# Sliding-window attention in a two-layer hybrid decoder step: TensorE's order of scores and probability transposes within a round

## Chip, cores, metric

One core of one Trainium2 chip. The metric is device microseconds of one launch of the whole kernel, median of the runs.

## What is computed

One inference step of a trunk of two layers (DEPTH = 2, D_MODEL = 1024). Layer 0 is grouped-query attention over a window of 128 keys, 16 query heads on 4 key heads of 64, with a learned sink per head, RMS-normed queries and keys and a relative-position bias. Layer 1 is an mLSTM. Each is followed by a squared-ReLU MLP of width 4096. The prompt has 16 meta tokens and 1024 tokens; a sample group has 8 sequences of 4 tokens with 128 cached keys and values each. The part that matters here:

```
s = einsum('...qkgd,...skd->...kgqs', qg, k) * hd**-0.5 + rel_bias(dist)
m = maximum(max(s), sink);  p = exp(s - m)
den = sum(p) + exp(sink - m)
o = einsum('...kgqs,...skd->...qkgd', (p / den), v)
```

Everything is float32; the large projections split each operand into a high and a low part (three matmuls in the place of one).

## The kernel before

All of it is one program on one core, with a hand-written instruction list for each engine and semaphores between them. The stages follow one another: load and norm, q/k/v projection, attention, output projection (`wo_pe`), MLP, mLSTM, MLP, store.

**The rounds.** Prompt attention has NG = 36 pieces, numbered n = 0 to 35: four steps of four heads each, and in each step nine query blocks (`block_of`, L732). Block 0 of a step is the 16 meta tokens (16 x 16 scores a head), block 1 sees 16 + 128 keys, the seven others are full: 128 queries by 256 keys a head. Below, S(n), T(n) and V(n) are TensorE's three kinds of work on piece n:

- S(n), `att_scores_pe` (L742): scores of four heads into PSUM banks 0/1 for even n, 2/3 for odd n. It first waits for `s_taken`: the softmax of piece n-2 has read these banks.
- T(n), `att_transpose_pe` (L763): eight transposes of the scaled probabilities into banks 4 and 5, which exist once. It waits for `prob_ready` of n and for `pT_ready` of n-1.
- V(n), `att_values_pe` (L777): sixteen matmuls probabilities times values into bank 6 or 7. It waits for `o_taken` of n-2 and for `pT_ready` of n. In rounds up to n = 8 it also carries two other transposes (`turns_pe`).

LAG = 4: in round n TensorE (`att_pe`, L814) issues T(n-4), S(n), V(n-5), in this order. The rounds run from 2 to 40; S(0) and S(1) come earlier, from `att_first_pe`. The two kinds of exception: T(0) stands behind S(4); and the sample group's cached keys are transposed in rounds 36 and 37 (`turn_k_pe` 0 and 1, then 2 and 3, L1005, four transposes each into banks 0 and 1), there behind T. Turns 2 and 3 wait until turns 0 and 1 have been copied out (`k_copied`), because they use the same banks. In round 38 `sample_scores_pe` (L1042) follows, behind T(34).

**The other engines, in order in round n.** VectorE (`att_dve`, L939): o(n-6), the two operations that take V(n-6)'s result (L907, L910, which signals `o_taken`); softmax(n), four score reads (L846, the last signals `s_taken`) and a sum (L852); den(n-1), sum and reciprocal (L871, L873). Softmax(n) waits for S(n) and, because the four probability buffers go round, for T(n-4). In round 18 `spread_dve` (L990) stands first. ScalarE (`att_act`, L919): pT(n-4), the copy of T(n-4) to SBUF (L890; L893 and L894 for small blocks), which signals `pT_ready`; exp(n-1), four exponentials and one for the sinks (L862, L864). In round 36 turn 1's copy follows exp(35) (L1025), and turn 0's copy follows den(35) on VectorE (L1020). GpSimd: the scaling by 1/den (L880), which signals `prob_ready`.

Behind attention `wo_pe` (L1169) waits for the last `o_taken`, does two groups of the projection, the transposes of the sample probabilities, another group, and then `sample_values_pe` (L1107): matmuls with 32 columns each (L1117), and the rest of the projection.

Of the kernel before, what the change touches and what calls it, by code (L numbers as in the profile page):

```python
# [137 lines left out]
def build(nc, a, out, scratch):  # L138

    with ExitStack() as ctx:  # L140
# [562 lines left out]
        NG = 4 * TILES  # L703
        P_BUFS = 4
        LAG, READY = 4, 2
# [20 lines left out]
        def prob_of(n, rows, k, cols):  # L726

            if n == 0:
                return prob_m[rows, k, cols.start - BLK:cols.stop - BLK]
            return (prob_1 if n == 1 else prob[p_buf(n)])[rows, k, cols]  # L730

        def block_of(n):  # L732

            step, b = divmod(n, TILES)
            if b == 0:
                return (COL_M, META), (0, None, 0), BLK, BLK + META, step
            col = BLK * (b - 1)
            if b == 1:
                return (col, BLK), (COL_M, None, META), BLK - META, 2 * BLK, step
            return (col, BLK), (col - BLK, b - 2, BLK), 0, 2 * BLK, step  # L740

        def att_scores_pe(pe, n):  # L742
            (qc, nq), (pc, _, npk), k0, k1, step = block_of(n)
            gp, ip = divmod(step, 2)
            if n >= 2:
                pe.wait_ge(s_taken, n - 1)
            for i in range(2):
                for par in range(2):
                    rows = slice(HD * par, HD * par + HD)
                    bank = 2 * (n % 2) + par  # L750
                    lhsT = q[rows, 4 * gp + 2 * ip + i, qc:qc + nq]
                    o = ps[0:nq, bank, 2 * BLK * i:2 * BLK * i + 2 * BLK]
                    if npk == BLK:
                        last = nc.tensor.matmul(o, lhsT, kn[rows, gp, pc:pc + 2 * BLK], start=True, stop=True)  # L754
                    else:
                        if npk:
                            nc.tensor.matmul(o[:, k0:BLK], lhsT, kn[rows, gp, pc:pc + npk],
                                             start=True, stop=True)
                        last = nc.tensor.matmul(o[:, BLK:k1], lhsT, kn[rows, gp, qc:qc + nq],
                                                start=True, stop=True)  # L760
            last.then_inc(s_done, 1)

        def att_transpose_pe(pe, n):  # L763
            (qc, nq), (pc, _, npk), k0, k1, step = block_of(n)
            pe.wait_ge(prob_ready, n + 1)
            if n >= 1:
                pe.wait_ge(pT_ready, n)
            for k in range(4):
                bank = 4 + k // 2
                for part, (c0, nk) in enumerate(((k0, npk), (BLK, nq))):  # L770
                    if nk:
                        o = ps[0:nk, bank, (k % 2) * 2 * BLK + part * BLK:][:, 0:nq]
                        last = nc.tensor.transpose(o, prob_of(n, slice(0, nq), k, slice(c0, c0 + nk)),  # L773
                                                   ident[0:nq, 0:nq])
            last.then_inc(t_done, 1)

        def att_values_pe(pe, n):  # L777
            (qc, nq), (pc, pt, npk), k0, k1, step = block_of(n)
            b = n % TILES
            gp, ip = divmod(step, 2)  # L780
            if n >= 2:
                pe.wait_ge(o_taken, n - 1)
            turns_pe(pe, n)
            if n == 0:
                pe.wait_ge(vmeta_done, 1)
            if n == 2 * TILES:
                pe.wait_ge(v_taken, V_TAKEN)
                pe.wait_ge(vmeta_done, 2)
            pe.wait_ge(pT_ready, n + 1)
            for i in range(2):  # L790
                for part, (t, nk) in enumerate(((pt, npk), (b - 1 if b else None, nq))):
                    for par in range(2):
                        cols = slice((2 * gp + par) * HD, (2 * gp + par) * HD + HD)
                        o = ps[HD * par:HD * par + HD, 6 + n % 2, BLK * i:BLK * i + nq]
                        v = v_tok[:, t, cols] if t is not None else v_meta[:, cols]
                        if nk:
                            last = nc.tensor.matmul(o, v, probT[0:nk, n % 2, 2 * par + i, part, 0:nq],  # L797
                                                    start=part == 0 or npk == 0, stop=part == 1)
            last.then_inc(pv_done, 1)
# [13 lines left out]

        def att_pe(pe):  # L814
            for n in range(2, NG + LAG + 1):
                if LAG < n < NG + LAG:
                    att_transpose_pe(pe, n - LAG)
                if NG <= n < NG + 2:
                    turn_k_pe(pe, 2 * (n - NG))
                    turn_k_pe(pe, 2 * (n - NG) + 1)  # L820
                if n == NG + 2:
                    sample_scores_pe(pe)
                if n == 3 * TILES:
                    pe.wait_ge(qk_normed, 30)
                if n < NG:
                    att_scores_pe(pe, n)
                if n == LAG:
                    pe.wait_ge(qk_ln, 30)
                    pe.wait_ge(out_free, V_LAST + 1)
                    att_transpose_pe(pe, 0)  # L830
                if n > LAG:
                    att_values_pe(pe, n - LAG - 1)

# [171 lines left out]
        def turn_k_pe(pe, j):  # L1005

            if j == 0:
                pe.wait_ge(kc_in, 64)
                pe.wait_ge(s_taken, NG - 1)
            elif j == 2:  # L1010
                pe.wait_ge(k_copied, 2)
            for i in range(4):
                b = 4 * (j % 2) + i
                last = nc.tensor.transpose(ps[:, j % 2, P * i:P * i + P],
                                           k_raw[:, b, P * (j // 2):P * (j // 2) + P], ident)
            last.then_inc(s_turns, 1)
# [25 lines left out]
        def sample_scores_pe(pe):  # L1042

            pe.wait_ge(s_taken, NG)
            pe.wait_ge(k_copied, 4)
            pe.wait_ge(q_spread, 5)
            for t in range(4):
                for c, ncol, keys in ((0, WIN, lambda gp, b: kcT[:, gp, b, :]),
                                      (WIN, SAMPLE, lambda gp, b: kn[:, gp, COL_S:COL_M])):
                    for gp in range(2):  # L1050
                        for half in range(2):
                            b = 2 * t + half
                            c0 = 256 * (t % 2) + c
                            o = ps[64 * half:64 * half + 64, 2 + t // 2, c0:c0 + ncol]
                            last = nc.tensor.matmul(o, q_big[:, gp, b, :], keys(gp, b), start=gp == 0, stop=gp == 1)
            last.then_inc(s_turns, 1)
# [1395 lines left out]
        @block.tensor  # L2452
        def _(pe):
            load_pe(pe)
            pe.wait_ge(gains_in, 48)
            pe.wait_ge(x_by_dve, 8)
            nc.tensor.transpose(ps[:, 7, 0:5 * KC], gain_rows[:, :], ident[0:5 * KC, 0:5 * KC]
                                ).then_inc(gains_t, 1)
            pe.wait_ge(line_in, 64)
            pe.wait_ge(rel_one, 1)  # L2460
            pe.wait_ge(x_by_act, 8)
            nc.tensor.matmul(ps[0:QH, 6, 0:LINE], rel_ext[:, :], bucket[:, :], start=True, stop=True
                             ).then_inc(line_mm, 1)
            qkv_pe(pe)
            att_pe(pe)
            wo_pe(pe)
            first_up_pe(pe, 0, U_MLP0, N_MLP0, h_hi, h_lo)
            mlp_slice_pe(pe, 0, U_MLP0, N_MLP0, 0, h_hi, h_lo, 1)
            with pe.Fori(1, SLICES) as i:
                mlp_slice_pe(pe, 0, U_MLP0, N_MLP0, i, h_hi, h_lo)  # L2470
            gates_pe(pe)
            in_pe(pe)
            chunks_pe(pe)
            out_pe(pe)
            first_up_pe(pe, 1, U_MLP1, N_MLP1, h_hi2, h_lo2)
            mlp_slice_pe(pe, 1, U_MLP1, N_MLP1, 0, h_hi2, h_lo2, 1)
            with pe.Fori(1, SLICES) as i:
                mlp_slice_pe(pe, 1, U_MLP1, N_MLP1, i, h_hi2, h_lo2)
            y_pe(pe)
# [35 lines left out]
```

## Time and profile before

| | us |
|---|---|
| median of 3 runs | 2419.23 |
| the three runs | 2418.41, 2419.23, 2890.8 |
| time of the profiled execution | 2418.44 |
| its span, first to last instruction | 2416.3 |
| TensorE busy | 2381.5 (99%) |
| VectorE busy | 1008.2 (42%) |
| ScalarE busy | 570.3 (24%) |
| GpSimd busy | 108.7 (4%) |

Times in the trace count from the first instruction. The profiled execution takes 2.1 us more than its span. Prompt attention runs from about 188 to 305 us of it. A row of the timeline can merge equal instructions: its first number is the start, its second the length.

### The profile page before, as it was taken

To read this page: it belongs to the slowest core of one execution; us is meant where nothing else is said; L and a number is where in the kernel's file an instruction comes from. 1 tells how busy PE (TensorE), PEld (TensorE's weight loads), DVE (VectorE), ACT (ScalarE), POOL (GpSimd) and SP (SyncE) were. 2 spreads that over 40 slices of the span, in tenths; PEclk is the share of its full clock that TensorE was granted. 3 is DMA by queue.
4 is the path that set the end of the run, shared out by engine and by line. 5 is a ranking of instruction groups with operands and counts; after the bars stand their busy time and mean duration, and the time that the engine had idled before them with its cause. 6 is when DMAs were issued, how large, how long until landed. Compare 5 with 4: busy or idle time off the path is not lost.

```text
span 2416.3 us, 35099 instructions
## 1 busy us (share of the span) xinstructions
PE 2381.5 (99%) x15129; PEld 2317.9 (96%) x15129; DVE 1008.2 (42%) x1390; ACT 570.3 (24%) x995; POOL 108.7 (4%) x123
## 2 busy tenths in 40 slices
PE   7999999999999999999999999999999999999998
PEld 7997799999999999999999998889999999999998
DVE  5448824433333333334623325545343343343333
ACT  5458822211111101112410015422111111110111
POOL 0004500000000000000000004100000000000000
PEclk9999999999999999999999999999999999999999
DMA  8613031111111111111231126441111111111111
GB/s 223 122 36 94 11 99 35 53 36 53 37 50 52 35 52 35 52 35 52 92 73 36 36 98 172 129 140 36 53 50 38 52 35 52 46 41 52 35 35 72
DMA packets 131074, 152.96 MB, mean 63 GB/s; under 512 B 33405, under 2 KB 105881, under 8 KB 130700
## 3 DMA queue, kind: packets, MB, share of 16 engines
q1 hardware_dynamic: 125132, 137.77, 19.4%
q0 software_dynamic: 3008, 13.60, 1.9%
q8 instruction: 65, 1.06, 0.2%
q10 hardware_dynamic: 2848, 0.34, 0.1%
q14 instruction: 21, 0.17, 0.0%
HBM read 126.50 MB, written 27.22 MB: 64 GB/s over the span
## 4 chain that ended last, share of the span: by engine, by line
PE 96%; DVE 2%; ACT 1%; DMA 1%; issue 0%; SPq 0%; DVEq 0%
PE ps L304 42%; PE ps L310 21%; PE ps L290 8%; PE ps L293 8%; PE ps L291 8%; PE ps L797 1%; PE ps L773 1%; PE ps L754 1%; ACT prob L862 1%; PE ps L1824 1%; PE ps L1164 1%; DMA x_tok<-in_x_prompt 1%; PE ps L1165 1%; PE ps L1166 1%; PE ps L1805 1%; PE ps L1809 1%
## 5 line engine op out<-in xcount | busy, mean ns | idle before, releaser
L1289 DVE TENSOR_TENSOR x<-x,ps 128x1074 f32<-128x1074 f32 (+1 forms) x128 | 161.9, 1265 | 460.7 <-PE ps L310 460.7
L258 ACT ACTIVATE w_hi<-raw 128x1024 fp32r<-128x1024 f32 x180 | 187.3, 1050 | 651.3 <-PE ps L310 484.9
L304 PE MATMUL ps<-act_hi,w_lo 128*128 128x358 f32 (+1 forms) x1536 | 334.0, 325 | 0.0
L304 PE MATMUL ps<-act_hi,w_hi 128*128 128x358 f32 (+1 forms) x1536 | 333.7, 325 | 0.0
L304 PE MATMUL ps<-h_hi,w_hi 128*128 128x358 f32 (+1 forms) x1536 | 333.4, 325 | 0.0
L304 PE MATMUL ps<-h_hi,w_lo 128*128 128x358 f32 (+1 forms) x1536 | 333.2, 325 | 0.0
L290 PE MATMUL ps<-h_hi,w_hi 128*128 128x358 f32 (+1 forms) x864 | 286.8, 332 | 4.4 <-DVE h_lo L352 2.6
L291 PE MATMUL ps<-h_lo,w_hi 128*128 128x358 f32 (+1 forms) x864 | 282.4, 327 | 0.0
L310 PE MATMUL ps<-act_lo,w_hi 128*128 128x358 f32 (+1 forms) x1536 | 272.1, 324 | 0.0
L1271 DVE SCALAR_TENSOR_TENSOR relu<-ps,rstd 128x1074 f32<-128x1074 f32 (+1 forms) x64 | 81.1, 1267 | 447.5 <-PE ps L310 447.5
L304 PEld LDWEIGHTS ps<-act_hi,w_hi 128*128 128x128 f32 x1536 | 264.0, 189 | 0.0
L304 PEld LDWEIGHTS ps<-act_hi,w_lo 128*128 128x128 f32 x1536 | 263.9, 189 | 0.0
L310 PE MATMUL ps<-h_lo,w_hi 128*128 128x358 f32 (+1 forms) x1536 | 263.6, 326 | 0.0
L304 PEld LDWEIGHTS ps<-h_hi,w_lo 128*128 128x128 f32 x1536 | 263.6, 189 | 0.0
L304 PEld LDWEIGHTS ps<-h_hi,w_hi 128*128 128x128 f32 x1536 | 263.4, 189 | 0.0
L310 PEld LDWEIGHTS ps<-h_lo,w_hi 128*128 128x128 f32 x1536 | 252.7, 189 | 1.3
L310 PEld LDWEIGHTS ps<-act_lo,w_hi 128*128 128x128 f32 x1536 | 253.1, 189 | 0.0
L1253 ACT ACTIVATE act_hi<-relu 128x1074 fp32r<-128x1074 f32 (+1 forms) x64 | 70.4, 1099 | 714.8 <-DVE relu L1271 714.8
L263 DVE TENSOR_TENSOR w_lo<-raw,w_hi 128x1024 fp32r<-128x1024 f32 x180 | 219.6, 1220 | 36.7 <-ACT w_hi L258 36.6
L293 PE MATMUL ps<-h_hi,w_lo 128*128 128x358 f32 (+1 forms) x864 | 189.2, 327 | 0.0
L290 PEld LDWEIGHTS ps<-h_hi,w_hi 128*128 128x128 f32 x864 | 163.2, 189 | 7.8 <-issue 7.2
L291 PEld LDWEIGHTS ps<-h_lo,w_hi 128*128 128x128 f32 x864 | 163.5, 189 | 0.4
(306 smaller groups left out, 2277.4 us busy)
## 6 DMA issues: line engine op xcount, KB each, us to landing
raw<-in_mlp_w_up SPq DMA_DIRECT2D x32, 1024.0 KB, 5.7
raw<-in_mlp_w_down SPq DMA_DIRECT2D x32, 1024.0 KB, 5.0
raw<-in_mlstm_w_in SPq DMA_DIRECT2D x12, 1024.0 KB, 5.3
scratch_x<-x SPq DMA_DIRECT2D x1, 4296.0 KB, 17.8
x<-scratch_x SPq DMA_DIRECT2D x8, 537.0 KB, 6.0
scratch_x<-x POOLq DMA_DIRECT2D x1, 4296.0 KB, 14.1
x<-scratch_x SPq DMA_DIRECT2D x8, 528.0 KB, 4.7
x_tok<-in_x_prompt SPq DMA_DIRECT2D x8, 512.0 KB, 12.0
```

What stands on the lines that cost most here:

```text
L258: nc.scalar.activation(unit_view(w_hi, slot, down), raw_unit(j, rslot, down), ACT.Copy).then_inc(w_hi_ready, 1)
L263: nc.vector.tensor_tensor(unit_view(w_lo, slot, down), raw_unit(j, rslot, down), unit_view(w_hi, slot, down).bitcast(F32), ALU.subtract).t ...
L290: nc.tensor.matmul(o, wh, hi[:, k_of, c], start=start, stop=False)
L291: nc.tensor.matmul(o, wh, lo[:, k_of, c], start=False, stop=False)
L293: last = nc.tensor.matmul(ps[:, bank + g, 0:w], wl, hi[:, k_of, g * w:g * w + w], start=False, stop=stop)
L304: nc.tensor.matmul(ps[:, bank + g, 0:width], w_block(w, slot, k, kc, cols), hi[:, k, g * width:g * width + width], start=start and i == 0, ...
L310: last = nc.tensor.matmul(ps[:, bank + g, 0:width], w_block(w_hi, slot, k, kc, cols), lo[:, k, g * width:g * width + width], start=False, ...
L754: last = nc.tensor.matmul(o, lhsT, kn[rows, gp, pc:pc + 2 * BLK], start=True, stop=True)
L773: last = nc.tensor.transpose(o, prob_of(n, slice(0, nq), k, slice(c0, c0 + nk)), ident[0:nq, 0:nq])
L1253: nc.scalar.activation(act_hi[:, j, t], relu[j % 2][:, t], ACT.Square).then_inc(up_done, 1)
L1271: nc.vector.scalar_tensor_tensor(out=view(relu[j % 2][:, :]), in0=ps[:, out_banks(n):out_banks(n) + 3, 0:w], scalar=0.0, in1=r, op0=ALU.ma ...
L1289: nc.vector.tensor_tensor(view(x[:, o, :]), view(x[:, o, :]), ps[:, out_banks(n):out_banks(n) + 3, 0:w], ALU.add).then_inc(out_free, 1)
```

## The change

Only TensorE's order inside a round changes. Before, round n issued T(n-4), [key turns], S(n), V(n-5). Now it issues [key turns], S(n), T(n-4), V(n-5). The sample scores of round 38 still stand behind T(34), and T(0) behind S(4). No instruction is added or removed, and the waits inside each piece stay as they are. The distance of four rounds between S and T (LAG) was there before.

```diff
         def att_pe(pe):
             for n in range(2, NG + LAG + 1):
-                if LAG < n < NG + LAG:
-                    att_transpose_pe(pe, n - LAG)
                 if NG <= n < NG + 2:
                     turn_k_pe(pe, 2 * (n - NG))
                     turn_k_pe(pe, 2 * (n - NG) + 1)
-                if n == NG + 2:
-                    sample_scores_pe(pe)
                 if n == 3 * TILES:
                     pe.wait_ge(qk_normed, 30)
                 if n < NG:
@@
                 if n == LAG:
                     pe.wait_ge(qk_ln, 30)
                     pe.wait_ge(out_free, V_LAST + 1)
-                    att_transpose_pe(pe, 0)
+                if LAG <= n < NG + LAG:
+                    att_transpose_pe(pe, n - LAG)
+                if n == NG + 2:
+                    sample_scores_pe(pe)
                 if n > LAG:
                     att_values_pe(pe, n - LAG - 1)
```

## Rows read from the trace of the kernel before

**Rows 1.** The page, part 4: the chain that ended last, shares of the span by engine.

```profile
PE 96%; DVE 2%; ACT 1%; DMA 1%; issue 0%; SPq 0%; DVEq 0%
```

**Rows 2.** Busy windows: stretch, us, PE, PEld, DVE, ACT, POOL busy, clock, DMA.

```profile
240.00:290.00 50.00, 49.01 (x522) 37.28 (x523) 47.57 (x231) 46.93 (x172) 29.62 (x27) 1.00 0.01 2
```

**Rows 3.** Timeline of one full round, three engines: start us, length us, engine, line.

```profile
285.77 1.09 PE L773 MATMUL ps<-cst,prob 128*128 128x128 f32 x8
...
286.80 1.13 PE L754 MATMUL ps<-kn,q 64*128 64x256 f32 x8
...
286.90 1.02 ACT L890 ACTIVATE probT<-ps 128x1024 f32<-128x1024 f32 x1
...
287.86 1.09 PE L797 MATMUL ps<-probT,v_tok 128*64 128x128 f32 x16
...
287.98 0.48 DVE L846 CUSTOM_DVE_ANT_0 prob<-ps,bias,nsinks 128x256 f32<-128x256 f32 x1
...
289.79 0.19 ACT L864 ACTIVATE esink<-stat 128x4 f32<-128x4 f32 x1
...
290.02 0.16 DVE L871 TENSOR_TENSOR stat<-stat,esink 128x4 f32<-128x4 f32 x1
```

**Rows 4.** Timeline, TensorE, opening of attention; in brackets idle before and its releaser.

```profile
193.72 1.03 PE L773 MATMUL ps<-cst,prob 128*16 128x128 f32 x8 [1.27 <-ACT probT L894]
...
196.73 1.07 PE L773 MATMUL ps<-cst,prob 128*128 128x128 f32 x8 [0.58 <-ACT probT L894]
...
197.73 1.14 PE L754 MATMUL ps<-kn,q 64*128 64x256 f32 x8
```

**Rows 5.** Timeline, VectorE and TensorE, round 19.

```profile
239.82 0.43 DVE L910 TENSOR_TENSOR o_lo<-ps,o_hi 128x256 fp32r<-128x256 f32 x1
...
240.30 1.09 PE L797 MATMUL ps<-probT,v_tok 128*64 128x128 f32 x16 [0.74 <-DVE o_lo L910]
```

**Rows 6.** Timeline, TensorE in rounds 24 and 28, VectorE in round 31.

```profile
252.46 1.06 PE L773 MATMUL ps<-cst,prob 128*128 128x128 f32 x8 [0.19 <-ACT probT L894]
...
265.03 1.06 PE L773 MATMUL ps<-cst,prob 128*128 128x128 f32 x8 [0.51 <-ACT probT L890]
...
276.65 0.47 DVE L846 CUSTOM_DVE_ANT_0 prob<-ps,bias,nsinks 128x256 f32<-128x256 f32 x1
```

**Rows 7.** Timeline of rounds 36 to 38, three engines.

```profile
288.88 1.09 PE L773 MATMUL ps<-cst,prob 128*128 128x128 f32 x8
...
289.81 1.04 PE L1014 MATMUL ps<-cst,k_raw 128*128 128x128 f32 x8
...
291.80 1.09 PE L773 MATMUL ps<-cst,prob 128*128 128x128 f32 x8
...
292.90 0.19 ACT L864 ACTIVATE esink<-stat 128x4 f32<-128x4 f32 x1
...
293.41 0.66 DVE L1020 COPY kcT<-ps 128x512 f32<-128x512 f32 x1
...
294.13 1.09 PE L1014 MATMUL ps<-cst,k_raw 128*128 128x128 f32 x8 [1.24 <-DVE kcT L1020]
...
296.18 1.09 PE L773 MATMUL ps<-cst,prob 128*128 128x128 f32 x8
```

**Rows 8.** Timeline, TensorE: the first matmul behind the longest idle; sample values.

```profile
27.06 0.40 PE L290 MATMUL ps<-h_hi,w_hi 128*128 128x358 f32 x1 [2.59 <-DVE h_lo L352]
...
318.85 1.97 PE L1117 MATMUL ps<-pcT,v_c 128*128 128x32 f32 x16
...
321.38 3.43 PE L1117 MATMUL ps<-pcT,v_c 128*128 128x32 f32 x16
```

**Rows 9.** Busy windows, columns as in rows 2: the stretches where the clock changes.

```profile
28.00:29.00 1.00, 1.00 (x5) 1.00 (x4) 1.00 (x2) 1.00 (x2) 0.00 (x0) 0.54 1.45 238
...
321.00:322.00 1.00, 1.00 (x6) 0.67 (x6) 0.00 (x0) 0.00 (x0) 0.00 (x0) 0.81 0.00 0
...
328.00:330.00 2.00, 2.00 (x12) 2.00 (x12) 0.09 (x1) 0.00 (x0) 0.00 (x0) 0.89 1.02 415
```

## The prediction

> **What bounds the kernel now.** I read the chain that ended last first: 96% of it is TensorE [rows 1], so time counts where TensorE's list of instructions gets longer or where it stands still. Then the busy windows of attention, since the change touches nothing else: of 50 us there, TensorE is busy 49.0, VectorE 47.6, ScalarE 46.9 [rows 2]. The reader is to see that this stage has three engines near their limit, so that a later start on one soon becomes a wait on another. Then the timeline of one full round [rows 3]. TensorE starts T at 285.77, S at 286.80, V at 287.86; with V as long as T, start to start, the round is 1.03 + 1.06 + 1.03 = 3.11 us. ScalarE starts the copy pT at 286.90, 1.13 after T's start; its last exponential starts at 289.79 and is done some 0.1 later, so ScalarE itself needs about 3.0 of the 3.11. VectorE starts the softmax at 287.98 and den at 290.02, where its own work is about 2.9. TensorE sets the pace of full rounds, with 0.1 to 0.2 us to spare on the others.
>
> **The cyclic part.** The list of TensorE becomes S(n), T(n-4), V(n-5). Nothing is added, so its own round stays 3.11 us. Against V, each S comes one T earlier (1.03) and each T one S later (1.06). What hangs on T moves with it: pT(n-4), behind it on ScalarE exp(n-1), behind that den(n-1), o(n-5) and softmax(n+1) on VectorE, all about 1.06 later against V. The round of the copy is not tighter: between T(n-4) and T(n-3) stand one S and one V in either order. What gets shorter is S's margin. Softmax(35) starts at 287.98 and has read its scores about 1.65 later (four reads of 0.40 and a tail), at 289.63. An S two rounds behind S(35) would start at 286.80 + 6.22 = 293.02: a margin of 3.4. From this the change takes 1.03 + 1.06 and leaves 1.3. V's margin behind o shrinks by 1.06 as well. In full rounds I therefore put the swap at 0 [rows 3]. If the margin were 1 us smaller than read, it would still be positive; below nothing it can't go, since TensorE doesn't stand still there now.
>
> **The opening.** T(1) waited 1.27 and T(2) 0.58 for probT, while S(5) and S(6) stood behind them [rows 4]. Now S(5) fills part of the first wait and S(6) all of the second: T(2) can't start before 196.73, since its copy is no earlier, but S(6), which came behind it at 197.73, is done by then. V(1) starts 1.06 earlier: -1.0 us. Bounds: 0 (S(6) itself waits for softmax(4)) and -1.8, both waits filled.
>
> **Round 18 and 19.** The lead does not last. V(14) stood 0.74 us and was let go by o_lo, which ran at 239.82 for 0.43 [rows 5]; that is o(12), late because `spread_dve` stands ahead of it. By then T, ScalarE and VectorE are at the same absolute times as before: the lead of 1.0 and the swap of 1.06 cancel for T. So V(14) starts at 240.3 in both kernels, with a longer wait before it: +1.0. From T(9) on I find T 0.2 late, since S(15) meets a small wait, and VectorE is late by the same: +0.2. Bounds -0.3 and +1.1 (the whole lag of VectorE, if the lead is lost earlier).
>
> **Short rounds.** Where T or V is short (blocks 0 and 1), TensorE's round falls to 2.3 us while the two others need 2.9 to 3.0, and two such rounds in a row use up S's margin of 1.3. There are two such places behind round 19. Round 24: T(20) waited 0.19 before [rows 6]; now S(24) waits about 0.4 for softmax(22): +0.2. Round 33: nothing waited; softmax(31) began at 276.65 [rows 6] and by my reckoning of the rounds begins 1.35 later, at 278.0, has read its scores at 279.65, where S(33) would be free to start at 279.3: +0.4. Round 28: T(24) waited 0.51 [rows 6]; now S(28) waits 0.5 instead: 0. Together +0.6; bounds -0.7 (all old waits gone, no new one) and +1.6.
>
> **Rounds 36 to 38.** Here the change has a price in its own right [rows 7]. The first two key turns (1.0) now stand ahead of T(32), which was at 288.88. The chain behind T(32) is fixed: its copy, exp(35), whose sink part was at 292.90, den(35), the copy of turn 0 at 293.41 (0.66), and then turns 2 and 3 at 294.13: 5.25 from T(32)'s start to turn 2. All of it moves by 1.0. Before, T(33) at 291.80 ran inside this stretch and turns 2 and 3 waited 1.24 after it. Now turns 2 and 3 head the round, and T(33), V(32) and all of TensorE are queued behind them: another 1.0. T(34) then comes only one V behind T(33), and the copy pT(33) between them takes 1.13 + 1.02, which is 0.1 to 0.2 more than T and V: +0.15. Sum +2.15; T(34), at 296.18 before, starts at 298.3 plus what came earlier. Bounds +1.0 (only T(32)'s delay counts) and +3.2 (a wait of its own for the fourth key copy ahead of the sample scores). TensorE's stall before turn 2 becomes 3.2 us where it was 1.24.
>
> **The clock.** The granted clock fell while `sample_values_pe` ran: 0.81 of full in 321 to 322, and back between 328 and 330 at 0.89 [rows 9], so half speed from about 321.6 to 328.4. The second L1117 group took 3.43 where the first took 1.97 [rows 8]: 1.5 lost, and about 1.8 more in the dense matmuls behind it, 3.3 together. The clock also fell behind idle time: 2.59 us of it before 27.06 [rows 8], then 0.54 in 28 to 29 [rows 9]. These sample matmuls are the same in the new kernel and only start 3 us later, so I carry the 3.3 over: 0. Bounds -3.3 (the fall doesn't come) and +3.4 (a second one comes).
>
> The Trainium skill, "TensorE: Matmul & The Clock Gate", section "Part 1: The HAM clock gate (the 'warmup' mystery)", speaks against the change: the half clock is the default state, and recent activity of TensorE is what releases it. By it the new 3.2 us stall in round 37 is a place where the clock can fall, and the sum would be higher by the price given in the second rival; by the windows of rounds 36 and 37 alone, it would not. The trace agrees with the rule in that 2.59 us of idle time was followed by half speed.
>
> **Sum.** -1.0 + 1.0 + 0.2 + 0.6 + 2.15 = +2.95, say +2.9. The profiled execution took 2418.44 (2.1 around its span of 2416.3), 0.8 below the median of 2419.23. 2418.44 + 2.9 = 2421.3 on its scale; the forecast for the median is 2419.23 + 2.9 = 2422.1 us. Everything behind attention is TensorE's list without a wait to hide in, so the delay goes through to the end.
>
> **Rivals.**
> 1. The sample values lose their clock fall. They start 3 us later, and the fall need not come at the new place; then the 3.3 us come back: 2422.1 - 3.3 = 2418.8, not slower than before. For it: the fall came only with the second half of these matmuls, so it may depend on where they lie. Against it: the stretch is as long and as thin as before. It decides from the point at which it gives back more than 2.9, that is when nearly all of the fall is gone. Chance 0.15.
> 2. The clock falls in round 37's stall. Half speed over the turns, T(33), V(32) and what follows, for half of or all the 6.8 us that the fall from 321.6 to 328.4 lasted, costs 1.7 to 3.4: 2423.8 to 2425.5. For it: rows 8 and 9 at 28 us. Against it: the stall has work right up to it and the turns right after it. Chance 0.13.
> 3. The end doesn't cost what I say, because the waits of rounds 36 and 37 overlap other than I read, and the opening's 1.0 survives round 19: 0 to +1, that is 2419.2 to 2420.2. For it: VectorE's margin at V(14) rests on 0.2 us. Against it: the chain T(32) to turn 2 is visible step by step. Chance 0.14.
> 4. It does not do what it says: excluded but for a few in a hundred, as only the list's order changes.
>
> **Chances and range.** My forecast, +1.5 to +4.3, has 0.56; the rest is in the rivals and 0.02 elsewhere. The range that takes in rival 1's value less closely and most of rival 2: 2418.3 to 2425.5. A difference of 2% is 48 us, about what a measurement of this kernel can tell from no change, and more than a third of the whole attention stage of 117 us; no case comes near it. Faster by over 2%: 0.01; within 2%: 0.98; slower by over 2%: 0.01.
>
> **What would show it.** Right: T(1) and T(2) near 194.0 and 196.7 but V(1) at 197.8; V(14) let go by o_lo at 240.3 to 240.5; new waits of S on L846 in rounds 24, 28, 33; turn 2 at 295.7 with a wait of some 3.2 on kcT; the projection's first matmul at about 308.3 where it was at 305.4; half clock again near 325. Wrong: full rounds longer than 3.11, V waiting for o in every round (then VectorE's lag was under-read), or a half clock within 290 to 305.

## The result, and the profile after

| | before | changed |
|---|---|---|
| median, us | 2418.41 (20 runs) | 2421.6 (20 runs) |
| lowest to highest, us | 2414.43 to 2890.8 | 2419.94 to 2423.43 |
| profiled execution, us (span) | 2418.44 (2416.3) | 2420.37 (2418.2) |
| from S(4)'s start to the projection's first matmul, us | 114.25 | 116.34 |

The ratio is 1.0014 [1.0008, 1.0021]: the changed kernel is slower, by 3.2 us in the medians, where +2.9 was forecast and 2422.1 us (range 2418.3 to 2425.5) stood on record. One run before, at 2890.8, is a slow one that neither the median nor the ratio counts, but it was one of the three runs behind the forecast's base of 2419.23, which lies 0.8 above the median of all. The profiled pair differs by only 1.93; a likely cause of that gap is shown further on (x11 and x12). In the rows of the changed kernel, the line numbers of everything behind `att_pe` in the file are one below those of before (L1013 is what L1014 was).

To compare two profiles stage by stage, one needs a mark inside them, since the start of attention moves from execution to execution: S(4) started at 191.12 before and at 190.98 here, and anywhere from 190.54 to 192.54 in the experiments. All "relative" times below are counted from S(4)'s start in the same profile.

The chain and the busy windows of the changed kernel, which answer to [rows 1, 2] (windows: stretch, us, PE, PEld, DVE, ACT, POOL busy, clock, DMA):

```profile
PE 95%; DVE 2%; ACT 1%; DMA 1%; issue 0%; SPq 0%; DVEq 0%
...
240.00:290.00 50.00, 48.91 (x523) 37.03 (x518) 46.17 (x222) 46.03 (x167) 29.39 (x27) 1.00 0.01 2
```

The three engines are as full as they were. The timeline of a full round, answering to [rows 3] (start, length, engine, line, in brackets the idle time before and its releaser):

```profile
285.71 1.13 PE L754 MATMUL ps<-kn,q 64*128 64x256 f32 x8
...
286.77 1.09 PE L773 MATMUL ps<-cst,prob 128*128 128x128 f32 x8
...
287.80 1.09 PE L797 MATMUL ps<-probT,v_tok 128*64 128x128 f32 x16
...
287.90 1.02 ACT L889 ACTIVATE probT<-ps 128x1024 f32<-128x1024 f32 x1
...
288.82 1.09 PE L1013 MATMUL ps<-cst,k_raw 128*128 128x128 f32 x8
```

From S at 285.71 to the next round at 288.82 is 3.11 us, as before. The copy starts 1.13 after its transpose, as before, and both stand one S later in the round.

The opening, TensorE, answering to [rows 4]:

```profile
192.79 1.13 PE L754 MATMUL ps<-kn,q 64*128 64x256 f32 x8 [0.50 <-DVE stat L845]
...
195.47 1.13 PE L754 MATMUL ps<-kn,q 64*128 64x256 f32 x8 [0.23 <-DVE stat L845]
...
197.59 0.43 PE L797 MATMUL ps<-probT,v_meta 16*64 16x128 f32 x4
```

The waits of T(1) and T(2), 1.27 and 0.58, have become waits of S(5) and S(6), 0.50 and 0.23. V(1) starts 6.61 behind S(4); before it was 7.67 (198.79). The lead is 1.06.

It doesn't stay at that. In rounds 7 to 12 TensorE also does the other transposes that V carries (`turns_pe`), ahead of V's own matmuls. This is round 8, T(4) and two of these (L618), in the kernel before:

```profile
203.74 1.09 PE L773 MATMUL ps<-cst,prob 128*128 128x128 f32 x8
...
205.83 0.44 PE L618 MATMUL ps<-cst,vT 128*128 128x128 f32 x2
```

And in the changed kernel, where nothing stands between them:

```profile
203.45 1.09 PE L773 MATMUL ps<-cst,prob 128*128 128x128 f32 x8
204.38 0.38 PE L618 MATMUL ps<-cst,vT 128*128 128x128 f32 x2
```

From T(4) to the next matmul it is 0.93 where it was 1.02, and from L618 to the next 0.31 where it was 0.36. Over these rounds TensorE's lead grows from 1.06 at V(1) to 1.93 at V(8) (28.78 behind S(4), before 30.71), with no wait in either kernel there. Then S(15) waits 0.34 for VectorE, a wait that was not there before.

Round 19, answering to [rows 5], and the three short rounds, answering to [rows 6]:

```profile
239.69 1.09 PE L797 MATMUL ps<-probT,v_tok 128*64 128x128 f32 x16 [1.79 <-DVE o_lo L909]
...
251.95 1.13 PE L754 MATMUL ps<-kn,q 64*128 64x256 f32 x8 [0.29 <-DVE stat L845]
...
264.58 0.41 PE L757 MATMUL ps<-kn,q 64*128 64x16 f32 x4 [0.51 <-DVE stat L845]
...
279.05 1.13 PE L754 MATMUL ps<-kn,q 64*128 64x256 f32 x8 [0.29 <-DVE stat L845]
```

TensorE reaches V(14) 1.52 earlier than before (46.92 behind S(4), before 48.44). There V(14) waits 1.79 for o_lo where it waited 0.74, and starts at 48.71, before 49.18: of the lead, 0.47 is left. The short rounds then eat it.

Rounds 36 to 38, answering to [rows 7]:

```profile
288.82 1.09 PE L1013 MATMUL ps<-cst,k_raw 128*128 128x128 f32 x8
...
289.75 1.04 PE L773 MATMUL ps<-cst,prob 128*128 128x128 f32 x8
...
293.76 0.19 ACT L863 ACTIVATE esink<-stat 128x4 f32<-128x4 f32 x1
...
294.27 0.66 DVE L1019 COPY kcT<-ps 128x512 f32<-128x512 f32 x1
...
294.99 1.09 PE L1013 MATMUL ps<-cst,k_raw 128*128 128x128 f32 x8 [3.18 <-DVE kcT L1019]
...
298.16 1.06 PE L773 MATMUL ps<-cst,prob 128*128 128x128 f32 x8 [0.18 <-ACT probT L889]
```

The key turns now start round 36 at 288.82, which is 97.84 relative; before, the round began with T(32) at 97.76: +0.08. Turn 2 waits 3.18 us where it waited 1.24, T(34) starts at 107.18 (before 105.06), and the projection starts 2.09 later than before.

The sample values, answering to [rows 8], and the windows of the clock, answering to [rows 9]:

```profile
323.33 2.74 PE L1116 MATMUL ps<-pcT,v_c 128*128 128x32 f32 x16
```

```profile
324.00:325.00 1.00, 1.00 (x8) 1.00 (x8) 0.00 (x0) 0.00 (x0) 0.00 (x0) 0.67 0.00 0
...
331.00:332.00 1.00, 1.00 (x7) 1.00 (x7) 0.00 (x0) 0.00 (x0) 0.00 (x0) 0.92 1.04 425
```

The granted clock is at half again, from about 324.3 to 331.2: 6.8 us, as before. From the projection's first matmul to the end the profiled execution takes 2420.37 - 307.32 = 2113.05, before 2418.44 - 305.37 = 2113.07.

### The profile page after: what moved, and what is told of

Same layout as the page of the kernel before. It is cut to its first block, busy times and chain, and to the rows that moved or that the text cites. A ratio compares the mean times of both kernels' runs of the same rounds, so it can differ in the third digit from the quotient of the medians.

```text
span 2418.2 us, 35099 instructions
## 1 busy us (share of the span) xinstructions
PE 2380.9 (98%) x15129; PEld 2317.8 (96%) x15129; DVE 1007.8 (42%) x1390; ACT 570.3 (24%) x995; POOL 108.9 (5%) x123
## 3 DMA queue, kind: packets, MB, share of 16 engines
q8 instruction: 65, 1.06, 0.2%
## 4 chain that ended last, share of the span: by engine, by line
PE 95%; DVE 2%; ACT 1%; DMA 1%; issue 0%; SPq 0%; DVEq 0%
PE ps L304 41%; PE ps L310 21%; PE ps L290 8%; PE ps L293 8%; PE ps L291 8%; PE ps L773 1%; PE ps L797 1%; PE ps L754 1%; ACT prob L861 1%; PE ps L1823 1%; DMA x_tok<-in_x_prompt 1%; PE ps L1163 1%; PE ps L1164 1%; PE ps L1165 1%; PE ps L1804 1%; PE ps L1808 1%
```

## The experiments

"Length" is the time from S(4) to the projection's first matmul. Half clock is added up over windows of 1 us, each with 2 x (1 - granted clock); the three places are at V(14)'s wait, at turn 2's wait, and in the sample values. "Rest" is the profiled time less the start of the projection. The number in brackets is the median of the kernel before on the same chip, in runs beside these. The ratio is formed from these runs too, but isn't the quotient of the two medians; differences of under 0.1% between medians are left alone below, and lengths are compared. Each length comes from one profile.

| kernel | median (before) | ratio | length | rest | half clock, three places |
|---|---|---|---|---|---|
| before | 2418.41 | | 114.25 | 2113.07 | 0, 0, 6.8 |
| changed | 2421.6 (2418.41) | 1.0014 [1.0008, 1.0021] | 116.34 | 2113.05 | 0, 0, 6.8 |
| x1 turns behind | 2417.84 (2419.05) | 1.0005 [0.9996, 1.0013] | 115.25 | 2111.49 | 0, 0, 3.4 |
| x2 turns ahead only | 2420.96 (2419.05) | 1.0011 [1.0002, 1.002] | 117.49 | 2113.07 | 0, 3.4, 6.8 |
| x3 swap to round 17 | 2417.85 (2419.05) | 0.9998 [0.9989, 1.0007] | 113.77 | 2113.03 | 0, 0, 6.8 |
| x4 copies first | 2418.22 (2419.05) | 0.9996 [0.9988, 1.0005] | 114.13 | 2113.17 | 0, 0, 6.8 |
| x7 ends in old order | 2419.68 (2418.86) | 1.0002 [0.9993, 1.0011] | 114.72 | 2113.14 | 0, 0, 6.8 |
| x5b values interleaved | 2416.32 (2418.86) | 0.9988 [0.9979, 0.9997] | 114.23 | 2110.02 | 0, 0, 0 |
| x8 before, copies first | 2416.45 (2418.86) | 0.9989 [0.998, 0.9998] | 112.77 | 2111.49 | 0, 0, 3.4 |
| x11 changed again | 2421.19 (2418.86) | 1.0011 [1.0002, 1.002] | 119.32 | 2111.51 | 3.4, 3.4, 3.4 |
| x12 changed, third | one run, 2421.86 | | 119.27 | 2111.50 | 3.4, 3.4, 3.4 |
| x13 changed, interleaved | 2420.42 (2418.13) | 1.0007 [0.9998, 1.0016] | 118.76 | 2109.96 | 0, 6.8, 0 |
| x10 clear on GpSimd | 2417.84 (2418.13) | 1.0 [0.9991, 1.0009] | 113.53 | 2112.96 | 0, 0, 6.8 |
| x9 parts together | 2413.04 (2418.13) | 0.9979 [0.997, 0.9988] | 112.11 | 2109.90 | 0, 0, 0 |

**x1: the changed kernel, key turns behind T again.**

```diff
-                if NG <= n < NG + 2:
-                    turn_k_pe(pe, 2 * (n - NG))
-                    turn_k_pe(pe, 2 * (n - NG) + 1)
...
                 if LAG <= n < NG + LAG:
                     att_transpose_pe(pe, n - LAG)
+                if NG <= n < NG + 2:
+                    turn_k_pe(pe, 2 * (n - NG))
+                    turn_k_pe(pe, 2 * (n - NG) + 1)
```

> The changed kernel with only the key turns of rounds 36 and 37 put back behind T; scores stay first in every round. Measure: time from the start of S(4) to the projection's first matmul, 114.25 us in the kernel before (191.12 to 305.37) and 116.34 in the changed one (190.98 to 307.32). Theory: the whole loss is the key turns' place, so 114.3 (within 0.3) and a median 0 to 0.5 us above the kernel before. Rival, the swap of S and T itself makes the rounds slower: the length stays at 115.5 or more.

Measured: 115.25, halfway between the 114.3 expected and the changed kernel's 116.34. Three rows of its timeline, TensorE and ScalarE:

```profile
290.52 1.06 PE L773 MATMUL ps<-cst,prob 128*128 128x128 f32 x8 [0.18 <-ACT probT L889]
...
295.21 0.20 ACT L863 ACTIVATE esink<-stat 128x4 f32<-128x4 f32 x1
...
296.44 1.09 PE L1013 MATMUL ps<-cst,k_raw 128*128 128x128 f32 x8 [1.89 <-DVE kcT L1019]
```

The last exponential's sink part stands at 295.21, relative 102.78. In the changed kernel it was at 293.76, relative 102.78 as well, and before at 101.78. So ScalarE's list ends 1.00 late whether or not the turns stand ahead of T(32). From the copy of T(31) at 289.35 on, ScalarE has no idle time in this kernel. It is late because T, and with it the copy, stands one S later in every round, and ScalarE needs about 2.97 of the 3.11 us of a round, so it can't make up 1 us in the rounds that are left. That delay reaches turn 2 by itself (104.01 relative, the same as in the changed kernel, 104.01). What the turns' place adds comes behind turn 2: T(33), which ran inside the wait here and takes 0.96 behind the turn in the changed kernel, and T(34)'s wait of 0.18; in the length, 116.34 - 115.25 = 1.09. V(32) stands behind turn 2 in both.

**x2: the order of before, key turns ahead of T.** The same four lines move, in the kernel before.

> The kernel before with only the key turns of rounds 36 and 37 put ahead of T; T stays ahead of S. Theory: 114.25 + 2.1 = 116.3 us from S(4) to the projection, turn 2 waits some 3.2 us for kcT, and the median is about 2 us above the kernel before. Rival, the loss needs the swap as well (VectorE and ScalarE late at round 36): under 115.3.

Measured: 117.49, more than the changed kernel has. The row of turn 2 and the window around it:

```profile
296.29 1.97 PE L1014 MATMUL ps<-cst,k_raw 128*128 128x128 f32 x8 [3.13 <-DVE kcT L1020]
```

```profile
296.00:298.00 2.00, 1.72 (x8) 1.72 (x9) 1.54 (x4) 0.00 (x0) 1.62 (x1) 0.50 0.00 0
```

Two things are in it. Turn 2 starts at 103.85, 0.84 later than before (103.01): here ScalarE does wait for T(32), 0.90 at 292.17, so the place of the turns alone makes almost the same delay that the swap alone makes in x1. The two don't add, because both end in the same chain. And the eight matmuls of the turn take 1.97 where they took 1.09: the granted clock is 0.50. From turn 2 to the projection it is 309.93 - 296.29 = 13.64, in the changed kernel 307.32 - 294.99 = 12.33: 1.3 for 3.4 us at half clock. Without these 1.3 the length is 116.2, as expected. This is the prediction's second rival, seen.

**x3: the new order in rounds 5 to 17, that of before from 18 on.**

```diff
-                if LAG < n < NG + LAG:
+                if 18 <= n < NG + LAG:
                     att_transpose_pe(pe, n - LAG)
...
-                    att_transpose_pe(pe, 0)
+                if LAG <= n < 18:
+                    att_transpose_pe(pe, n - LAG)
```

> New order in rounds 5 to 17 only, old order from round 18 on, key turns as in the kernel before. Theory: V(1) starts 1.06 us earlier against S(4), the wait of V(14) for o_lo in round 19 grows from 0.74 to about 1.3, so only about 0.5 us of the lead is left behind it, and the later small waits are the old ones: 113.8 us from S(4) to the projection. Rival, all of the lead is lost in round 19: 114.25; rival, all is kept: 113.2.

Measured: 113.77, as expected. The wait of V(14) is 0.88 and of turn 2 the old 1.23:

```profile
241.11 1.09 PE L797 MATMUL ps<-probT,v_tok 128*64 128x128 f32 x16 [0.88 <-DVE o_lo L911]
...
294.94 1.09 PE L1015 MATMUL ps<-cst,k_raw 128*128 128x128 f32 x8 [1.23 <-DVE kcT L1021]
```

V(14) starts 48.71 behind S(4), the very place of the changed kernel. The 0.47 that the opening leaves there goes through to the projection (114.25 - 113.77 = 0.48). In the time it is no difference that can be told (0.9998). Everything that the change costs comes behind V(14) in round 19.

**x4: the changed kernel, the copies of the key turns ahead of the exponential and the sums of round 35** (`turn_k_act` before `att_exp_act`, `turn_k_dve` before `att_den_dve`, in rounds 36 and 37). VectorE's part of the edit; ScalarE's is of the same form:

```diff
+                if n == NG:
+                    turn_k_dve(dve, 0)
                 if READY < n <= NG:
                     att_den_dve(dve, n - 1)
-                if NG <= n < NG + 2:
-                    turn_k_dve(dve, 2 * (n - NG))
+                if n == NG + 1:
+                    turn_k_dve(dve, 2)
```

> The changed kernel, but the copies of the key turns stand ahead of exp(35) on ScalarE and ahead of den(35) on VectorE. Theory (turns 2 and 3 wait 3.2 us only because both copies stand behind the softmax of piece 35): the wait falls to about 1.0, T(34) starts 2.1 us earlier against S(4), and the length is 114.2 us. Rival (T(34) is then held by exp(35), den and the scaling, which now start 0.6 later): 115 or more.

Measured: 114.13, 2.21 less than the changed kernel:

```profile
294.09 1.09 PE L1017 MATMUL ps<-cst,k_raw 128*128 128x128 f32 x8 [1.00 <-DVE kcT L1023]
```

The wait of turn 2 falls from 3.18 to 1.00. It was the place of the copy in two queues, not the copy, that cost the time.

**x7: the new order in rounds 5 to 33 only, and the turns behind T.** The diff is that of x3 with 34 for 18.

> The changed kernel with the key turns behind the transposes again (as in x1_turns_behind) and with the old order of a round (transposes, then scores) from round 34 on; rounds 5 to 33 keep the new order. It tells apart why T(32) still came late in x1 although the key turns were out of its way. If ScalarE is a round's part late there because T(31) stands behind S(35) (the swap itself), the old order at the end gives it back: turn 2 comes some 1 us earlier against S(4) than in x1 (about 103.1 us behind it, x1 104.0), and the time from S(4) to the projection is about 114.3 us. Rival: the delay has been made before round 34 and stays, turn 2 at 104.0 and 115.2 us as in x1.

Measured: between the two, 114.72, turn 2 at 103.49.

```profile
293.07 0.19 ACT L865 ACTIVATE esink<-stat 128x4 f32<-128x4 f32 x1
...
294.30 1.09 PE L1015 MATMUL ps<-cst,k_raw 128*128 128x128 f32 x8 [1.64 <-DVE kcT L1021]
```

ScalarE's last exponential is at 102.26, 0.48 late where x1 had 1.00. T(32) is back at its old place (97.84, before 97.76), so TensorE no longer delays anything here, yet half of the lag is still there: it has built up on ScalarE in the rounds before. The sink part of piece 32 stands 0.78 late (93.37 behind S(4), before 92.59), and three pieces later 0.48 of that is left, since a round has only some 0.14 us of slack. The direction is the first theory's, the size is half. The lag belongs to the swap; it is a debt that is paid back slowly.

**x8: the kernel before, with the copies first,** the edit of x4 alone.

> The kernel before with the copies of the last two key turns issued ahead of the exponential and the row sums of round 35 instead of behind them; the order on TensorE is untouched. In x4 the same edit on the changed kernel took 2.2 us from its wait of turn 2. If the wait of turn 2 before (1.24 us) is the same copy queue, it goes and the time from S(4) to the projection is about 113.0 us (before 114.25), so 1.2 us less. Rival: exp(35) moved behind the copies makes T(35) late by as much, and nothing is gained (114.2 us).

Measured: length 112.77, which is 1.48 less than before. Of the 2.4 by which the median is lower, the rest may be the sample values, which in this profile had 3.4 us at half clock and not 6.8. The wait of turn 2 is gone from TensorE's timeline:

```profile
294.14 1.04 PE L1018 MATMUL ps<-cst,k_raw 128*128 128x128 f32 x8
```

**x5b: the kernel before, the narrow sample-values matmuls between wide ones.**

```diff
-            group_pe(pe, U_WO + 1, N_WO + 1, 0, o_hi, o_lo, TG)
-            sample_values_pe(pe)
-            group_pe(pe, U_WO + 1, N_WO + 1, 1, o_hi, o_lo, TG)
+            group_pe(pe, U_WO + 1, N_WO + 1, 0, o_hi, o_lo, TG,
+                     lambda k: sample_values_pe(pe, k - 4) if k >= 4 else None)
+            group_pe(pe, U_WO + 1, N_WO + 1, 1, o_hi, o_lo, TG,
+                     lambda k: sample_values_pe(pe, k + 4) if k < 4 else None)
```

`group_pe` calls the function behind each of its k-steps, and each call issues four of the narrow matmuls (the first of a half also its wide opening one).

> The kernel before with the narrow sample-values matmuls (L1117) spread between the projection's wide matmuls instead of standing in two blocks; the sums are the same. It measures the clock's fall by itself, which both kernels have and which rival 1 of the prediction said the change might take away. If the run of narrow matmuls lets the clock fall, no window of 318 to 330 us shows half clock and the time is about 3.3 us less than before (2415.3). Rival: the fall has another cause (the projection's own start), the clock falls at the same place and the time is that of before within 0.5 us.

Two rows of its timeline and the window over the whole stretch; the same window of the kernel before had a granted clock of 0.76:

```profile
318.34 0.63 PE L1119 MATMUL ps<-pcT,v_c 128*128 128x32 f32 x4
...
319.38 0.53 PE L1119 MATMUL ps<-pcT,v_c 128*128 128x32 f32 x4
```

```profile
316.00:330.00 14.00, 14.00 (x91) 12.88 (x91) 2.24 (x6) 1.94 (x5) 0.00 (x0) 1.00 0.19 59
```

By the profile TensorE is busy for all 14.00 us in either kernel, so the clock fell there without idle time: it fell in the run of matmuls of 32 columns, and with wide ones between them it did not. "Rest" shrinks from 2113.07 to 2110.02, by 3.05, near the expected 3.3; the median shrinks by 2.5. What both kernels pay is settled by this, and the price too: the profiles with 3.4 us at half clock in this stretch have 2111.5, those with 6.8 have 2113.1, those with none 2110.0, so 1.5 us for every 3.4.

**x11 and x12: the changed kernel again.**

> The changed kernel once more, on the same chip as the runs beside it: the prediction's +2.9 us against what the profiled pair showed (+1.9) and the medians (+3.2). By the profiled pair: ratio about 1.0008, time from S(4) to the projection 116.3 us, full clock behind turn 2's 3.2 us wait. Rival: the wait of 3.2 us sometimes lets the clock fall, as in x2; then the execution is about 1.3 us longer again, with turns 2 and 3 and T(33) at half clock.

> The changed kernel, a third profile. The first had full clock behind both long waits (V(14) 1.79 us, turn 2 3.18 us) and 6.8 us at half clock at the sample values; the second had half clock behind both waits for 3.4 us each and 3.4 us at the sample values. If the fall behind a wait is a matter of chance in each execution, this one lies anywhere between: attention 116.3 us plus 1.3 to 1.7 for each fall. Rival: the second was an exception, and this one is 116.3 us.

Timeline of x11, TensorE, V(14) and turn 2, and of x12 the same two:

```profile
239.69 1.98 PE L797 MATMUL ps<-probT,v_tok 128*64 128x128 f32 x16 [1.79 <-DVE o_lo L909]
...
296.59 1.09 PE L1013 MATMUL ps<-cst,k_raw 128*128 128x128 f32 x8 [3.18 <-DVE kcT L1019]
```

```profile
239.81 1.97 PE L797 MATMUL ps<-probT,v_tok 128*64 128x128 f32 x16 [1.80 <-DVE o_lo L909]
...
296.63 1.09 PE L1013 MATMUL ps<-cst,k_raw 128*128 128x128 f32 x8 [3.18 <-DVE kcT L1019]
```

Busy windows of x11 behind both waits:

```profile
240.00:242.00 2.00, 2.00 (x18) 1.67 (x16) 1.90 (x14) 1.37 (x9) 1.22 (x1) 0.50 0.00 0
...
298.00:300.00 2.00, 2.00 (x14) 1.67 (x15) 0.00 (x0) 0.70 (x1) 0.00 (x0) 0.50 0.00 0
```

The waits are those of the first profile, to 0.01 us. Behind both of them the clock is at half for 3.4 us. V(14) takes 1.98 instead of 1.09, and S(24) comes at 62.57, where the first profile has 60.97: 1.6 lost. From turn 2 to the projection x11 takes 13.70, the first profile 12.33: another 1.37. The sample values lose their clock for 3.4 us and not 6.8, which gives back 2113.05 - 2111.51 = 1.54. The sum is 1.6 + 1.37 - 1.54 = +1.43, and x11's profiled time is 2421.8 against 2420.37: +1.43. The three terms together are the whole difference between the two executions, so nothing else differs. The changed kernel has at least two kinds of execution, and the first profile was of the cheaper one.

**x13: the changed kernel with the sample values interleaved.**

> The changed kernel with the sample values spread between the wide matmuls as in x5b. It leaves the falls behind the two long waits as the only ones. If these are there in some executions, the gain is what x5b had on the kernel before (2.5 us in the median) and the gap between the two kernels stays at the 2.3 to 3.2 us of the medians: 2418.9. Rival (the first rival of the prediction, by another way): the changed kernel's falls and the sample values' fall stand in for one another, and the gain is half as much, 2420.

Turn 2, and the window behind it:

```profile
294.58 1.97 PE L1013 MATMUL ps<-cst,k_raw 128*128 128x128 f32 x8 [3.18 <-DVE kcT L1019]
```

```profile
294.00:300.00 6.00, 5.42 (x32) 4.85 (x32) 1.97 (x4) 1.53 (x3) 1.89 (x1) 0.50 0.00 0
```

The sample values keep their clock, but in this execution the clock falls at turn 2's wait for 6.8 us, the first 1.2 of them inside the wait, and from there to the projection it is 14.72 instead of 12.33: 2.39 lost. The median lies at the rival's 2420, not at 2418.9: 0.8 us under x11's, on another chip. It fits that the falls stand in for one another, but the times of the two kernels overlap (2416.98 to 2421.82, and 2419.84 to 2423.07), so it is not shown.

**x10: x3 with the clearing of q_big moved to GpSimd.**

```diff
-            nc.vector.memset(q_big[:, :, :, :], 0.0).then_inc(q_spread, 1)
...
+                if n == 9:
+                    pool.wait_ge(out_ready, 12)
+                    nc.gpsimd.memset(q_big[:, :, :, :], 0.0).then_inc(q_spread, 1)
```

> The kernel of x3 (new order in rounds 5 to 17) with the clearing of q_big moved from VectorE's list in round 9 to GpSimd's. It tells what V(14) waits for. If VectorE's extra work ahead of round 18 (the clearing and the spreading) is what eats the opening's lead, its wait before V(14) in x3 (0.88 us) shrinks by the time of the clearing and the lead survives: 112.9 us from S(4) to the projection, where x3 had 113.8. Rival: V(14)'s wait comes from spread_dve alone, whose own 2 us stand directly ahead of o(12); then it stays 0.88 and 113.8.

Measured: V(14) still waits 0.63 (0.88 in x3), and the length is 113.53, 0.24 less, so the expectation failed and its rival is nearly true. GpSimd and VectorE in x3, then in x10:

```profile
237.41 1.89 POOL L881 TENSOR_TENSOR prob<-prob,stat 128x1024 f32<-128x1024 f32 x1 [1.22 <-DVE stat L874]
...
237.54 0.91 DVE L996 MEMSET q_big<- 128x1024 f32 x1 [0.16 <-issue]
...
238.49 1.65 DVE L1004 COPY q_big<-q 64x128 f32<-64x128 f32 x4
```

```profile
235.75 0.20 DVE L1003 COPY q_big<-q 64x128 f32<-64x128 f32 x1
...
235.87 1.89 POOL L881 TENSOR_TENSOR prob<-prob,stat 128x1024 f32<-128x1024 f32 x1 [1.22 <-DVE stat L874]
...
235.98 2.37 DVE L1003 COPY q_big<-q 64x128 f32<-64x128 f32 x3
```

The 0.91 of the clearing went, but the copies behind it grew: one of 0.20 and three of 2.37 together, where four took 1.65. In x10 three of them start at 235.98, beside GpSimd's scaling, and end 0.59 behind its end (238.35 against 237.76), which is three times 0.20. In x3 the four start at 238.49, while the scaling still runs (237.41 to 239.30), and end 0.84 behind its end (240.14), about four times 0.20. So the copies made next to no headway while the scaling ran, and it is its end that sets theirs. The clearing lay inside the scaling and had been filling a time that the copies could not use; what x10 gains, 0.25 in the wait and 0.24 in the length, fits the one copy that came ahead of the scaling. The Trainium skill, "GPSIMD Engine Reference", section "1. Specifications", says that GpSimd's way to SBUF is shared with VectorE for some of VectorE's instructions; the rows agree for these copies, and show no hold of the clearing, which took 0.91 and ended while the scaling ran.

**x9: what paid, together**: the order of x3, the copies first, x10's clearing and x5b's interleaving, on the kernel before.

> What the single runs say should add up, on the kernel before: the new order in rounds 5 to 17 only (x3: attention 0.5 us shorter), the copies of the last key turns first (x8: 1.5 us shorter), the clearing of q_big on GpSimd instead of VectorE (untried: the 0.7 to 0.9 us wait of V(14)), the sample values between the wide matmuls (x5b: 2.5 us in the median). Sum 5.2 to 5.4: 2413.6 us where the kernel before has 2418.9, and 111.4 us from S(4) to the projection. Rival: with V(14)'s wait gone, another stage is late there (VectorE's lag comes out as a wait of V or S a few rounds on) and the last term is nothing: 2414.4 and 112.3 us.

Measured: 2413.04, the ratio 0.9979 [0.997, 0.9988], 5.1 us faster than before, and 8.2 under the changed kernel's median in x11 (on another chip). The length, 112.11, is the rival's: the single gains 0.48 + 1.48 + 0.24 give 112.05. The one term that failed is the clearing. No window of attention or of the sample values is below full clock.

## Why the prediction was right, and where not

The total was right: +2.9 against +3.2 (+2.3 in x11's runs). Part of that is luck: the terms of attention came to +2.09, not +2.95, and half clock behind the long waits, which the sum put at 0, fills the gap in some executions.

**The cyclic part, at 0:** right for the full rounds, which stayed at 3.11, and no V waited for o in them (the three parts 1.03, 1.06 and 1.03 as printed add to 3.12; from T to T it is 3.11). Wrong for rounds 7 to 12. "Nothing is added, so its own round stays" took the length of TensorE's list to be independent of its order, but with T next to the other transposes the list got 0.87 shorter. Its direct effect ends at S(15) and V(14), which wait for VectorE, whatever TensorE has in hand; only that T(4) came 0.15 earlier by it has a part in the 0.47 below.

**The opening, -1.0:** right, -1.06.

**Round 18 and 19, +1.0 and +0.2:** the step that failed. It said that V(14) starts at the same time in both kernels; it starts 0.47 earlier against S(4). The prediction took it that "T, ScalarE and VectorE are at the same absolute times as before". But before, ScalarE had stood still twice, waiting for a T that a long V (with two other transposes in it) had made late. Two rows of the kernel before, ScalarE:

```profile
204.87 1.03 ACT L890 ACTIVATE probT<-ps 128x1024 f32<-128x1024 f32 x1 [0.29 <-PE ps L773]
...
208.35 1.02 ACT L890 ACTIVATE probT<-ps 128x1024 f32<-128x1024 f32 x1 [0.40 <-PE ps L773]
```

In the changed kernel ScalarE has no wait of that size there: T(4) comes 0.15 earlier against S(4), and T(5), which has only the short S(9) ahead of it, 1.17 earlier. Behind that stretch ScalarE is 0.67 ahead (the next sink part at 19.45, before 20.12), VectorE is 0.72 ahead when it lets go S(15), and from there on T is 0.46 ahead, where the prediction had it 0.2 late. Those 0.69 us are the likely source of the 0.47; this is read from the two timelines and was not tried by itself. The whole term measured +0.59, predicted +1.2. That V(14)'s wait grew by 1.05, as good as the 1.0 said, is chance: TensorE came 1.52 early and not 1.06, and V(14) started 0.47 early and not at the same time.

**Short rounds, +0.6:** right in the sum, from -0.47 to +0.08, +0.55. Singly: S(24) waits 0.29 (0.4 said), S(28) 0.51 (0.5 said), S(33) 0.29 (0.4 said).

**Rounds 36 to 38, +2.15:** +2.04 by T(34), the stall 3.18 (3.2 said). Right in size, but the reason given for the first 1.0 was one of two, either of which is enough. The prediction moved the chain from T(32) over its copy, exp(35) and den(35) to the copy of turn 0 because the turns stand ahead of T(32). x1 shows that the chain is 1.00 late without them, on ScalarE, by the swap; x2 shows that they alone make it 0.84 late. Whoever takes the swap to be free, as the term of the cyclic part says, would expect x1 to give 114.3, and so did I: it gave 115.25. The swap costs nothing per round, but leaves ScalarE one S late, and this is charged where the list ends. What comes behind turn 2, the second 1.0 and the 0.15, measured 1.09; it is T(33) and the wait of T(34), for V(32) stands behind turn 2 in the kernel before too.

**The clock, 0, and rivals 1 and 2:** 0 in the first profile; in x11 and x12 +1.6 + 1.4 - 1.5. The second rival, to which I gave 0.13, occurred in four of the five executions seen with a wait of 3.1 to 3.2 us before turn 2 (x2, x11, x12, x13, not the first profile), and in two of the three of the changed kernel itself. The prediction had named "a half clock within 290 to 305" as a sign of being wrong, and that sign came: 297.7 to 301.1 in x11. It had not looked at V(14), whose wait it had growing to some 1.7 us, as a place for a fall, and that fall cost 1.6. The price per fall was over-read: 1.37 for 3.4 us and 2.39 for 6.8, of which 1.2 lay inside the wait itself, where 1.7 and 3.4 stood. The median stayed under the 2423.8 of this rival because the other terms were smaller and the sample values gave back. The first rival came half true in the same executions: 1.5 of its 3.3 came back. The prediction treated the two as alternatives, and here they came together. The +2.09 of attention and the clock's +1.4 make +3.5 in such executions.

**The measure.** The prediction put at 2% what a measurement of this kernel can tell from no change. The interval of the ratio is 0.13% wide, and the change of 0.14% is clear of it.

**Rival 3** (0 to +1): half of it was so, the opening's lead partly survived round 19, but the end cost what was said. Nothing speaks for rival 4.

What stays open: how often each kind of execution occurs in the 20 timed runs, which have no trace (their mean granted clock is on record to 0.001, which is 4.8 us at half clock, too coarse to tell); whether the fall at V(14) and the one at turn 2 depend on one another; and why S(4) starts up to 2 us earlier or later from one profile to the next, which concerns the stages before the change.

## What to carry to other kernels

A reordering that leaves every round as long as it was can still make another engine late by one step, if that engine has little slack per round; the debt shows only where the list ends or changes, so walk the last rounds on that engine too. TensorE's own list can change length too, by what stands next to what. Before moving TensorE's instructions around a wait, look at what stands ahead of the operation that ends the wait in the other engines' queues: here moving the copies ahead gave 1.5 to 2.2 us, more than any order of TensorE's own list that was tried. A wait of TensorE can cost more than its length where half clock follows it (1.3 to 2.4 us here), and one profile doesn't show whether it does: take several, and compare them from a mark inside the stage.

## What the runs showed of the hardware

**The clock behind a wait.** Behind a wait of 3.1 to 3.2 us in attention the granted clock was half in four of five profiles; behind V(14)'s wait of 1.8 us in two of seven (x11, x12; not in the first profile, x1, x4, x7, x13); behind waits of 0.6 to 1.9 us at these two places in none of the others. Each fall lasted 3.4 or 6.8 us. At turn 2 it began 1.2 us before the end of the wait in x13, 0.7 before it in x2, and 1.1 behind it in x11. The same kernel differs from execution to execution. The Trainium skill, "TensorE: Matmul & The Clock Gate", section "Part 1: The HAM clock gate (the 'warmup' mystery)", says of the slow matmuls at a kernel's start that their number varies between runs of one kernel. The three profiles of the changed kernel show the like in its middle, with 6.8 us at half clock in one and 10.3 us in two.

**The clock without any wait.** TensorE, by the profile busy 14.00 of 14.00 us, went to half clock in a run of matmuls of 32 columns, and kept full clock when four of them at a time stood between matmuls of 358 columns. That is worth 3.05 us here, with no work removed.

**Two falls may share.** Where two falls of 3.4 us came earlier, the sample values' fall lasted 3.4 instead of 6.8 (x11, x12). It was also 3.4 in x1 and x8, which had no earlier fall, so the one need not cause the other.

**Transposes next to one another.** Eight transposes of 128x128 (L773) took 1.02 us to the next matmul with scores behind them, and 0.93 with other transposes behind them (T(4) of both kernels; the key turns and T in round 36 of both kernels, too, took 0.93). No run tried this by itself.

**VectorE's copies beside GpSimd's scaling.** Copies of 64x128 fp32 on VectorE made next to no headway while GpSimd's TENSOR_TENSOR over 128x1024 ran (1.89 us): in all five kernels read for this (before, changed, x3, x9, x10) they end 0.59 us behind it where three were left and 0.84 to 0.85 where four were, at 0.20 each. The clearing of 128x1024 (0.91) ended inside it.
